# Prompt scores from high and low parts, decode rows regrouped, and memory updates of two batch elements side by side

## The chip, the cores and the metric

The program runs on one core of a Trainium2 chip. The metric is the device time of one launch in microseconds (us), the median of three runs. TensorE (PE) does the matrix products, VectorE (DVE), ScalarE (ACT) and GpSimd (POOL) do the elementwise work, and SyncE (SP) issues most of the DMAs. Each engine takes its instructions in order. They are tied together by semaphores: an instruction adds to one, and another engine waits until it has reached a number.

## The reference

One decoder layer for 256 prompt tokens and 8 x 4 decode tokens (288 columns in all), model width 2048, in fp32. Only the second sub-layer matters here:

```
x += 1/2 * post_norm(SwiGLU_1(pre_norm(x)))
p  = pre_norm(x) @ w_in           # q, k, v, o of 4 heads x 256, two GLU halves, gates
mLSTM per head: s = (q k^T) * w_intra        # prompt: 256 x 256; decode: 4 x 4 in each batch element
                h = (s v + (q C) * w_inter) / max(|den|, exp(-m))
                C_new = g_state * C + sum_s g_keys k_s v_s^T      # decode: for each of 8 batch elements
conv:  GLU -> causal depthwise conv (31 taps) -> LayerNorm -> swish
x += post_norm(concat[heads, conv] @ w_out)
x += 1/2 * post_norm(SwiGLU_2(pre_norm(x)))
```

## The kernel before

**The stream.** Everything is held feature-major: 128 features on the partitions, 288 tokens along a row. All weights come as 654 pieces of 128 x 1024 in four slots. For a piece, ACT makes its high part `whi` (rounded to fp32r, L910), and DVE or POOL makes the rest `wlo` by a subtraction (`split_lo`: L1330 on DVE, L1860 on POOL; `DVE_LO` at L105 says which pieces of the middle stage are DVE's). PE multiplies each 128 x 128 block in three products: high by high, high by low, low by high (L473 to L475, `multiply`). 24 of these make one piece. A tile of the result (two pieces in the middle stage) lies in one of four PSUM banks until DVE takes it out (`evict`, L1515), and PE must find the bank free when it starts the tile four further on.

**The middle stage.** For each piece p of it, PE, ACT, DVE and POOL each run a list written out by hand. For head h the place is k = p - `KEYS_AT[h]`, with `KEYS_AT` = 8, 30, 54, 78. On PE, `between(p, j)` puts small products behind block j of piece p, here written (k, j). On DVE the order within a piece is: evict, LayerNorm part, head part, gate part, convolution part, and the split last. ACT's is: split, then the parts. Heads 1 and 2 have the same pattern. In head 0, the convolution's taps (L1624) run on DVE up to k = 13. In head 3, the LayerNorm steps of the conv channels run beside it (`ln_part`, `ln_squares` on PE, L780).

**One head.** The tiles k0, k1, v0, v1, q0, q1 come at k = 0 to 11. At k = 8 ACT copies the decode columns of keys and values four times side by side (`kv4`, L1158), so that 128 partitions hold four copies of the 32 decode rows. PE turns them (k = 9). At k = 10 ACT and at k = 11 DVE make of these copies high and low parts `k4`, `v4`: rows of one copy hold the high part, rows of another the low part (L1169 to L1171, L1674, L1678), and a product over all 128 rows then gives the sum of the products of parts. At k = 12 and 13 ACT makes `vm`: for each of 8 batch elements the values with all other rows zeroed (L1189). At k = 12 DVE evicts q1 and weights the queries (`qw`, `qwn`, L1687 to L1696). PE's `scores` follow at (13, 5), (13, 1), (13, 1), (13, 3) in heads 0 to 3: four fp32 products for the prompt, two of 256 columns and two of 128, each recorded as two instructions (L687), and two products of 32 columns for the decode tokens (L690). `query_memory` (L705) multiplies into four groups of 32 columns of the array, 16 fp32 products recorded as 32. `attend` (L728) waits among others for DVE's L1717.

**The memory update.** `update_memory(h, b)` multiplies `k4` by `vm` of batch element b: two fp32r products over all 128 rows, of 256 columns each (L744), into bank 7 or 4 in turn. It runs eight times, three blocks apart from (16, 1) to (18, 6), in head 0 two pieces later and in head 3 three (`LATE`). It waits until the bank's last content, two updates back, is out. DVE adds each to the memory `C` (L1737): numbers 0, 1, 2 at k = 16, 3 and 4 at k = 17, 5, 6, 7 at k = 18 (plus `LATE`), always behind that piece's `evict`.

## Time and profile before

| | |
|---|---|
| median of three runs | 2156.44 us (2156.44 to 2157.05) |
| the profiled execution | 2157.24 us, of which the span of the trace is 2155.5 us |
| instructions | 41798 |
| PE busy | 2149.3 us, 16278 products |
| DVE, ACT, POOL busy | 972.9, 895.1, 961.7 us |
| granted TensorE clock | 1.00 |
| DMA | 376.63 MB, mean 175 GB/s |

The busy time of an engine is the union of its instructions' durations. A product on PE overlaps the next, so its duration (some 0.30 us for 288 columns) is not what it costs; the distance from its start to the next start is (0.13 us). The timeline gives start, duration, engine, line and operation. Where one engine runs several instructions of one line in a row, they stand as one row with their count. "[... <- X]" is the idle time before it and what ended it.

### The profile page before, as it was taken

The numbers are of one execution on the slowest core, as the hardware profiler recorded it, in microseconds if no ns is written. First come the engines' busy times: TensorE is split into PE (matmuls) and PEld (weight loads), VectorE is DVE, ScalarE is ACT, GpSimd is POOL, SyncE is SP. The second block draws the span as 40 slices with busy tenths as digits, with TensorE's granted clock in tenths as the row PEclk, the third lists the DMA queues.
The fourth block names the chain that finished last, engine by engine and source line by source line (L and its number), as shares of the span: only waits on it lengthen the run. The fifth ranks groups of instructions, "written<-read, shape, count | busy, mean of one in ns | idle before, by whom it ended". The sixth has DMA issues, their size and how long they took to land.

```text
span 2155.5 us, 41798 instructions
## 1 busy us (share of the span) xinstructions
PE 2149.3 (100%) x16278; PEld 2138.5 (99%) x16278; DVE 972.9 (45%) x1406; ACT 895.1 (42%) x1159; POOL 961.7 (45%) x563
## 2 busy tenths in 40 slices
PE   9999999999999999999999999999999999999999
PEld 9999999999999999999999999999999999999998
DVE  6533432223434224987659738533432223333323
ACT  6434333333343335644345446433333333333443
POOL 1444443334444445466756332444443334444444
PEclk9999999999999999999999999999999999999999
DMA  7454555455555554656656544545455545554653
GB/s 249 165 168 163 165 166 172 159 165 168 167 164 162 170 169 146 208 191 229 239 191 226 194 160 148 172 160 171 156 172 168 167 157 170 162 172 157 210 164 129
DMA packets 104692, 376.63 MB, mean 175 GB/s; under 512 B 11640, under 2 KB 15868, under 8 KB 103584
## 3 DMA queue, kind: packets, MB, share of 16 engines
q1 hardware_dynamic: 97632, 349.00, 49.0%
q10 hardware_dynamic: 6848, 26.37, 3.5%
q8 instruction: 62, 1.02, 0.2%
q14 instruction: 22, 0.18, 0.0%
q0 software_dynamic: 128, 0.07, 0.0%
HBM read 360.21 MB, written 15.18 MB: 174 GB/s over the span
## 4 chain that ended last, share of the span: by engine, by line
PE 99%; DVE 1%; issue 0%; ACT 0%; POOL 0%; DVEq 0%; POOLq 0%
PE bank L475 30%; PE bank L473 30%; PE bank L474 30%; PE bank L528 1%; PE bank L535 1%; PE bank L539 1%; PE bank L833 1%; PE bank L835 1%; PE bank L834 1%; PE bank L546 0%; PE bank L744 0%; PE bank L770 0%; PE bank L687 0%; DVE wlo L1330 0%; DVE prod L1636 0%; PE bank L728 0%
## 5 line engine op out<-in xcount | busy, mean ns | idle before, releaser
L1860 POOL TENSOR_TENSOR wlo<-raw,whi 128x1024 fp32r<-128x1024 f32 x331 | 796.6, 2408 | 850.5 <-ACT whi L910 770.7
L473 PE MATMUL bank<-xh,whi 128*128 128x288 f32 x3344 | 992.1, 297 | 0.0
L474 PE MATMUL bank<-xl,whi 128*128 128x288 f32 x3344 | 988.3, 296 | 0.0
L475 PE MATMUL bank<-xh,wlo 128*128 128x288 f32 x3344 | 986.4, 295 | 0.0
L910 ACT ACTIVATE whi<-raw 128x1024 fp32r<-128x1024 f32 x652 | 687.3, 1056 | 604.8 <-PE bank L475 560.8
L1330 DVE TENSOR_TENSOR wlo<-raw,whi 128x1024 fp32r<-128x1024 f32 x323 | 467.7, 1449 | 771.2 <-ACT whi L910 769.9
L473 PEld LDWEIGHTS bank<-xh,whi 128*128 128x128 f32 x3344 | 630.2, 188 | 2.4 <-issue 2.2
L475 PEld LDWEIGHTS bank<-xh,wlo 128*128 128x128 f32 x3344 | 629.8, 188 | 0.0
L474 PEld LDWEIGHTS bank<-xl,whi 128*128 128x128 f32 x3344 | 628.7, 188 | 0.2
L475 PE MATMUL bank<-hh,wlo 128*128 128x288 f32 x1408 | 417.4, 296 | 0.0
L473 PE MATMUL bank<-hh,whi 128*128 128x288 f32 x1408 | 416.1, 296 | 0.0
L474 PE MATMUL bank<-hl,whi 128*128 128x288 f32 x1408 | 410.5, 292 | 0.0
L474 PEld LDWEIGHTS bank<-hl,whi 128*128 128x128 f32 x1408 | 268.4, 191 | 0.0
L473 PEld LDWEIGHTS bank<-hh,whi 128*128 128x128 f32 x1408 | 264.5, 188 | 0.0
L475 PEld LDWEIGHTS bank<-hh,wlo 128*128 128x128 f32 x1408 | 263.8, 187 | 0.0
L1883 POOL TENSOR_TENSOR scr<-scr 128x288 f32<-128x288 f32 x88 | 74.7, 849 | 208.7 <-ACT scr L999 208.7
L1003 ACT ACTIVATE hh<-scr 128x288 f32 (+1 forms) x88 | 39.1, 444 | 275.6 <-DVE scr L1468 275.6
L999 ACT ACTIVATE scr<-scr 128x288 f32<-128x288 f32 x88 | 39.2, 445 | 220.7 <-DVE scr L1447 220.7
L1447 DVE TENSOR_TENSOR scr<-bank,rstd 128x288 f32<-128x288 f32 x176 | 80.3, 456 | 77.1 <-PE bank L475 72.3
L1624 DVE SCALAR_TENSOR_TENSOR bank<-upad,vec,bank 128x256 f32<-128x256 f32 x232 | 92.8, 481 | 0.1
L1873 POOL TENSOR_TENSOR ssq<-ssq,sq 128x288 f32<-128x288 f32 x45 | 36.5, 812 | 79.3 <-ACT sq L1060 54.2
L1470 DVE TENSOR_TENSOR hl<-scr,hh 128x288 f32 (+1 forms) x88 | 40.3, 458 | 64.0 <-ACT hh L1003 64.0
(265 smaller groups left out, 1271.4 us busy)
## 6 DMA issues: line engine op xcount, KB each, us to landing
raw<-stream SPq DMA_DIRECT2D x654, 512.0 KB, 3.5
C<-c_in ACTq DMA_DIRECT2D x4, 2048.0 KB, 8.2
cs_out<-C ACTq DMA_DIRECT2D x4, 2048.0 KB, 7.9
late_kv<-late ACTq DMA_DIRECT2D x1, 2048.0 KB, 13.5
y_out<-x_res SPq DMA_DIRECT2D x7, 288.0 KB, 2.2
bc<-row_copy ACTq DMA_DIRECT2D x4, 448.0 KB, 8.6
conv_out<-upad ACTq DMA_DIRECT2D x4, 302.0 KB, 5.0
upad<-conv_in ACTq DMA_DIRECT2D x4, 272.0 KB, 3.4
```

Of the source, the lines that this page charges most:

```text
L473: pe.matmul(out, wh, mov_hi[:, k, :], start=first, stop=False)
L474: pe.matmul(out, wh, mov_lo[:, k, :], start=False, stop=False)
L475: return pe.matmul(out, wl, mov_hi[:, k, :], start=False, stop=last)
L910: act.activation(whi[:, g % SLOTS, :], raw[:, g % SLOTS, :], ACT.Copy).then_inc(hi_ready, 1)
L999: act.activation(scr[:, 2, :], scr[:, f % 2, :], ACT.Sigmoid).then_inc(sig_ready, 1)
L1003: act.activation(hh[:, k, :], scr[:, 4, :], ACT.Copy).then_inc(h_hi, 1)
L1330: dve.tensor_tensor(wlo[:, g % SLOTS, :], raw[:, g % SLOTS, :], whi[:, g % SLOTS, :].bitcast(F32), ALU.subtract).then_inc(lo_ready[g % SLO ...
L1447: ins = dve.tensor_tensor(out, src, rstd[:, :], ALU.mult)
L1470: dve.tensor_tensor(hl[:, k, :], scr[:, 4, :], hh[:, k, :].bitcast(F32), ALU.subtract)\
L1624: ins = dve.scalar_tensor_tensor(out=out, in0=up_prompt(j, SEQ, k), scalar=w, in1=acc, op0=ALU.mult, op1=ALU.add)
L1860: pool.tensor_tensor(wlo[:, g % SLOTS, :], raw[:, g % SLOTS, :], whi[:, g % SLOTS, :].bitcast(F32), ALU.subtract).then_inc(lo_ready[g % SL ...
L1883: pool.tensor_tensor(scr[:, 5 + f % 2, :], scr[:, f % 2, :], scr[:, 2, :], ALU.mult)\
```

## The change

The scores of the prompt take high and low parts of keys and queries: ACT writes the high parts `qk_hi` (`keep_high`, keys at k = 8, queries at k = 12), DVE subtracts them in place (`keep_low`, keys at k = 10, queries at k = 12), and PE makes three fp32r products for each fp32 product before. The copies of the decode rows are laid out per batch element (16 rows each: four copies of four tokens) in place of four copies of all 32. High and low rows are then told by masks `side` and `colv`, made once ahead, and the parts of `k4` and `v4` come from one instruction each over all rows. `vm` has two entries in place of eight, each with one batch element in every group of 32 rows. The update takes two batch elements at a time, each with a product over its own 32 rows, in two groups of array rows, four times in a head. Constants on POOL and DVE ahead of the heads, and the split of one small DMA into two, go with it.

```diff
+PAR = NB // Q_GROUP
+COPIES = P // NS
+UPDATE_ORDER = (0, 2, 1, 3, 4, 6, 5, 7)
...
             def scores(h):
                 pe.wait_ge(tile_evicted, tile_of(h, "q1") + 1)
                 pe.wait_ge(dec_lo, h + 1)
-                k, q = qkvo[:, 1, :, :], qkvo[:, 0, :, :]
+                for n in range(2):
+                    pe.wait_ge(qk_low[n], h + 1)
                 for lo, n, s, l in ((0, SEQ, 0, 0), (SEQ, P, P, P)):
                     for c in range(DC):
-                        pe.matmul(bank[7][:, lo:lo + n], k[:, c, s:s + P], q[:, c, l:l + n], start=(c == 0),
-                                  stop=(c == DC - 1))
+                        for m, (ks, qs) in enumerate(((qk_hi, qk_hi), (qk_hi, qk_lo), (qk_lo, qk_hi))):
+                            pe.matmul(bank[7][:, lo:lo + n], ks[:, 1, c, s:s + P], qs[:, 0, c, l:l + n],
+                                      start=(c + m == 0), stop=(c == DC - 1 and m == 2))
...
-            def update_memory(h, b):
-
-                if b < 2:
-                    pe.wait_ge(den_ready if b == 0 else qc_evicted, h + 1)
+            def update_memory(h, n):
+
+                if n:
+                    pe.wait_ge(cu_evicted, NB * h + 2 * n)
                 else:
-                    pe.wait_ge(cu_evicted, NB * h + b - 1)
-                pe.wait_ge(vm_ready, NB * h + b + 1)
-                out = bank[4 if b % 2 else 7]
+                    pe.wait_ge(den_ready, h + 1)
+                    pe.wait_ge(qc_evicted, h + 1)
+                    pe.wait_ge(vm_ready, PAR * (h + 1))
                 for c in range(DC):
-                    mm = pe.matmul(out[:, c * DH:(c + 1) * DH], k4[:, c * P:(c + 1) * P], vm[:, b, :],
-                                   start=True, stop=True)
-                mm.then_inc(cu_done, 1)
+                    for b in UPDATE_ORDER[2 * n:2 * n + 2]:
+                        g, r = divmod(b, PAR)
+                        own_rows = slice(NS * g, NS * (g + 1))
+                        mm = pe.matmul(bank[4 if g % 2 else 7][:, c * DH:(c + 1) * DH], k4[own_rows, c * P:(c + 1) * P],
+                                       vm[own_rows, r, :], start=True, stop=True, tile_position=(NS * g, 0))
+                        if c == DC - 1:
+                            mm.then_inc(cu_done, 1)
...
-            updates = {(16, 1): 0, (16, 4): 1, (16, 7): 2, (17, 2): 3, (17, 5): 4, (18, 0): 5, (18, 3): 6, (18, 6): 7}
+            updates = {(16, 1): 0, (16, 7): 1, (17, 5): 2, (18, 3): 3}
...
-                act.dma_start(row_copy[:, R_GK:ROWS], rowg[:, 0:TOK]).then_inc(rows_stored, 16)
+                act.dma_start(row_copy[:, R_GK:R_GK + SEQ], rowg[:, 0:SEQ]).then_inc(rows_stored, 16)
+                act.dma_start(row_copy[:, R_GK + SEQ:ROWS].rearrange("h (b t) -> h b t", t=NT),
+                              in_copies(rowg[:, SEQ:SEQ + P])[:, :, 0, :]).then_inc(rows_stored, 16)
...
+            def keep_high(h, n):
+
+                act.wait_ge(tile_evicted, tile_of(h, ("q1", "k1")[n]) + 1)
+                if h:
+                    act.wait_ge(sc_done, h)
+                act.activation(qk_hi[:, n, :, :], qkvo[:, n, :, 0:SEQ], ACT.Copy).then_inc(qk_high[n], 1)
...
                     for n in range(2):
-                        last = act.activation(kv4[:, n, :, :].rearrange("p c (j t) -> p c j t", j=P // NS),
-                                              four(qkvo[:, 1 + n, :, SEQ:TOK]), ACT.Copy)
+                        for c in range(DC):
+                            last = act.activation(in_copies(kv4[:, n, c, :]), copied(
+                                qkvo[:, 1 + n, c, SEQ:TOK].rearrange("p (b t) -> p b t", t=NT)), ACT.Copy)
                     last.then_inc(kv4_ready, 1)
+                    keep_high(h, 1)
...
-                if k in (12, 13):
-
+                if k == 12:
+
+                    keep_high(h, 0)
                     act.wait_ge(dec_lo, h + 1)
                     act.wait_ge(mask_ready, 1)
-                    for b in range(4 * (k - 12), 4 * (k - 11)):
-                        act.activation(vm[:, b, :], v4[:, :].bitcast(F32), ACT.Copy, scale=mask[:, b:b + 1])\
+                    for r in range(PAR):
+                        act.activation(vm[:, r, :], v4[:, :].bitcast(F32), ACT.Copy, scale=mask[:, r:r + 1])\
                            .then_inc(vm_ready, 1)
...
+                    dve.wait_ge(side_ready, 1)
+                    for n in range(2):
+                        last = dve.tensor_scalar(colv[:, n, :], col[:, 5, :], side[:, n, 1:2], None, ALU.mult)
+                    last.then_inc(colv_ready, 1)
+                    dve.wait_ge(colv_ready, 1)
                 if k == 11:
 
                     dve.wait_ge(dec_hi, h + 1)
-                    for r in (NS, 3 * NS):
-                        dve.scalar_tensor_tensor(out=v4[r:r + NS, :], in0=bank[7][r:r + NS, 0:DH],
-                                                 scalar=col[r:r + NS, 5, h:h + 1], in1=v4[r:r + NS, :].bitcast(F32),
-                                                 op0=ALU.mult, op1=ALU.subtract)
-                    half = slice(2 * NS, P)
-                    dve.tensor_tensor(k4[half, :], bank[7][half, DH:2 * DH], k4[half, :].bitcast(F32), ALU.subtract)\
-                       .then_inc(dec_lo, 1)
+                    dve.scalar_tensor_tensor(out=v4[:, :], in0=bank[7][:, 0:DH], scalar=colv[:, 0, h:h + 1],
+                                             in1=v4[:, :].bitcast(F32), op0=ALU.mult, op1=ALU.add)
+                    dve.scalar_tensor_tensor(out=k4[:, :], in0=bank[7][:, DH:2 * DH], scalar=side[:, 0, 0:1],
+                                             in1=k4[:, :].bitcast(F32), op0=ALU.mult, op1=ALU.add).then_inc(dec_lo, 1)
+                if k == 10:
+
+                    dve.wait_ge(kg_ready, h + 1)
+                    dve.wait_ge(kv4_ready, h + 1)
+                    keep_low(h, 1)
...
+                    for r in range(PAR):
+                        w = bc[:, h % 2, R_WI:R_GK].rearrange("p (g r t) -> p r g t", r=PAR, t=NT)[:, r, :, :].unsqueeze(1)
+                        last = dve.tensor_tensor(
+                            qw[:, :, r, n * r:n * (r + 1)].rearrange("p c (g t) -> p c g t", t=NT),
+                            qkvo[:, 0, :, SEQ:TOK].rearrange("p c (g r t) -> p c r g t", r=PAR, t=NT)[:, :, r, :, :],
+                            w.broadcast_to([P, DC, Q_GROUP, NT]), ALU.mult)
...
                     dve.tensor_tensor(qwn[:, 0, :], qwn[:, 0, :], qwn[:, 1, :], ALU.add).then_inc(qw_ready, 1)
+                    keep_low(h, 0)
...
-                for b in ((0, 1, 2), (3, 4), (5, 6, 7))[first] if 0 <= first < 3 else ():
-                    dve.wait_ge(cu_done, NB * h + b + 1)
-                    src = bank[4 if b % 2 else 7][:, :]
+                for n in ((0, 1), (2, 3), (4, 5, 6, 7))[first] if 0 <= first < 3 else ():
+                    dve.wait_ge(cu_done, NB * h + n + 1)
+                    b = UPDATE_ORDER[n]
+                    src = bank[4 if b // PAR % 2 else 7][:, :]
...
+            def keep_low(h, n):
+
+                dve.wait_ge(qk_high[n], h + 1)
+                dve.tensor_tensor(qk_lo[:, n, :, 0:SEQ], qkvo[:, n, :, 0:SEQ], qk_hi[:, n, :, :].bitcast(F32),
+                                  ALU.subtract).then_inc(qk_low[n], 1)
```

## Rows read from the trace of the kernel before

**Rows 1.** The profile's page: busy time, share of the span, instructions

```profile
PE 2149.3 (100%) x16278; PEld 2138.5 (99%) x16278; DVE 972.9 (45%) x1406; ACT 895.1 (42%) x1159; POOL 961.7 (45%) x563
```

**Rows 2.** Waits of PE: engine, line, waited for: us in total, times, longest

```profile
PE bank L728 <- DVE sq L1717: 0.4, 2, 0.2
```

**Rows 3.** Groups of PE instructions by form: form, count | busy us, mean ns | idle

```profile
L744 PE MATMUL bank<-vm,k 128*128 128x256 f32 x64 | 12.7, 279 | 0.0
...
L744 PEld LDWEIGHTS bank<-vm,k 128*128 128x128 f32 x64 | 10.2, 188 | 0.0
...
L705 PEld LDWEIGHTS bank<-C,qw 128*32 128x32 f32 x128 | 3.7, 109 | 2.7 <-issue 0.7
```

**Rows 4.** Timeline of PE at the scores of head 0

```profile
930.07 1.47 PE L687 MATMUL bank<-qkvo 128*128 128x256 f32 x8
931.38 0.53 PE L690 MATMUL bank<-qkvo,cpr 128*128 128x32 f32 x4
```

**Rows 5.** Timeline of PE at the first update of head 0

```profile
950.43 0.39 PE L744 MATMUL bank<-vm,k 128*128 128x256 f32 x2
950.67 0.29 PE L473 MATMUL bank<-xh,whi 128*128 128x288 f32 x1
```

**Rows 6.** Timeline of PE around the column-grouped products of head 0

```profile
941.32 0.29 PE L475 MATMUL bank<-xh,wlo 128*128 128x288 f32 x1
941.54 1.93 PE L705 MATMUL bank<-C,qw 128*32 128x256 f32 x32
943.41 0.40 PE L473 MATMUL bank<-xh,whi 128*128 128x288 f32 x1
943.65 0.29 PE L474 MATMUL bank<-xl,whi 128*128 128x288 f32 x1
```

**Rows 7.** One line each: durations ns min/median/max, first and last start, forms

```profile
L1330 DVE TENSOR_TENSOR wlo<-raw,whi x323: 1160/1227/2579, 12.1 to 2126.8; 128x1024 fp32r<-128x1024 f32 x162
L1177 ACT ACTIVATE vtok<-bank x4: 579/580/599, 922.6 to 1173.9; 128x512 f32<-128x512 f32 x4
L1687 DVE TENSOR_TENSOR qw<-qkvo,bc x4: 225/226/1829, 927.2 to 1179.6; 128x64 f32<-128x64 f32 x4
```

**Rows 8.** Timeline of DVE, head 0: before its taps, and k = 10 to 12

```profile
901.63 0.99 DVE L1621 TENSOR_SCALAR bank<-upad,vec 128x256 f32<-128x256 f32 x2 [3.02 <-POOL upad L1995]
...
918.75 3.22 DVE L1624 SCALAR_TENSOR_TENSOR bank<-upad,vec,bank 128x256 f32<-128x256 f32 x8
...
926.72 0.46 DVE L1536 TENSOR_TENSOR qkvo<-bank,rstd 128x288 f32<-128x288 f32 x1
```

**Rows 9.** Timeline of POOL: ahead of the heads, and head 0 at k = 10

```profile
884.76 7.08 POOL L1860 TENSOR_TENSOR wlo<-raw,whi 128x1024 fp32r<-128x1024 f32 x3 [28.81 <-DVE y L1436]
...
918.67 4.79 POOL L1860 TENSOR_TENSOR wlo<-raw,whi 128x1024 fp32r<-128x1024 f32 x2
```

**Rows 10.** Timeline of DVE, head 3, k = 12: eviction of q1, and what follows `qwn`

```profile
1179.07 0.46 DVE L1536 TENSOR_TENSOR qkvo<-bank,rstd 128x288 f32<-128x288 f32 x1
...
1180.26 1.22 DVE L1330 TENSOR_TENSOR wlo<-raw,whi 128x1024 fp32r<-128x1024 f32 x1
```

**Rows 11.** Timeline of PE: scores and first update of head 1, scores of head 3

```profile
1007.21 1.47 PE L687 MATMUL bank<-qkvo 128*128 128x256 f32 x8
...
1023.27 0.40 PE L744 MATMUL bank<-vm,k 128*128 128x256 f32 x2
...
1179.96 1.47 PE L687 MATMUL bank<-qkvo 128*128 128x256 f32 x8
```

**Rows 12.** Timeline of DVE: head 1 at k = 12 and 18, head 0 at k = 18

```profile
1003.44 0.46 DVE L1536 TENSOR_TENSOR qkvo<-bank,rstd 128x288 f32<-128x288 f32 x1 [2.77 <-PE bank L475]
...
1030.94 0.46 DVE L1525 TENSOR_TENSOR scr<-bank,rstd 128x288 f32<-128x288 f32 x1 [0.76 <-POOL upad L1995]
1031.32 0.74 DVE L1737 SCALAR_TENSOR_TENSOR C<-C,bc,bank 128x512 f32<-128x512 f32 x1
...
954.40 1.22 DVE L1330 TENSOR_TENSOR wlo<-raw,whi 128x1024 fp32r<-128x1024 f32 x1
```

More of the change, by code:

```diff
@@ L228, in hybrid_layer_kernel @@
         ml = place("ml", [P, D_MLSTM // P, TOK], F32R)
+        qkvo_at = arena[0]
         qkvo = place("qkvo", [P, 4, DC, TOK])
+        qk_lo = place("qk_lo", [P, 2, DC, TOK], F32R, qkvo_at)
         yc = place("yc", [P, CC, TOK])
@@ L272, in hybrid_layer_kernel @@
         ntmp = place("ntmp", [P, DC, NB])
-        mask = place("mask", [P, NB])
+        mask = place("mask", [P, PAR])
+        side = place("side", [P, 2, 2])
+        colv = place("colv", [P, 2, H])
         qwn = place("qwn", [P, DC, NS])
@@ L346, in hybrid_layer_kernel @@
         cap_ready, cap_added = sem("cap_ready"), sem("cap_added")
+        qk_high, qk_low = [sem(f"qk_high{n}") for n in range(2)], [sem(f"qk_low{n}") for n in range(2)]
+        low_ready, side_ready, colv_ready = sem("low_ready"), sem("side_ready"), sem("colv_ready")
         turn_ready, sums_ready = sem("turn_ready"), sem("sums_ready")
@@ L800, in between @@
                         attend(h)
-                    b = updates.get((k - LATE[h], j))
-                    if b is not None:
-                        update_memory(h, b)
+                    n = updates.get((k - LATE[h], j))
+                    if n is not None:
+                        update_memory(h, n)
                 if (p, j) == (MIX_FROM, 3):
@@ L1136, in head_part @@
                 if h == 0 and k == 6:
[L1138 removed]
+                    act.wait_ge(rows_stored, 48)
                     spread_rows(0)
@@ L1607, in _ @@
             dve.wait_ge(cap_ready, 1)
-            dve.tensor_reduce(ntmp[:, 0, :].rearrange("p (r j) -> p r j", j=Q_GROUP), own, AX_X, ALU.add)
+            dve.tensor_reduce(ntmp[:, 0, :].rearrange("p (g r) -> p g r", r=PAR), own, AX_X, ALU.add)
             link(dve.tensor_reduce(turn[:, 1:2], cap[:, :], AX_X, ALU.max))
@@ L1611, in _ @@
             dve.tensor_scalar(turn[:, 1:2], turn[:, 1:2], 0.0, None, ALU.is_ge).then_inc(turn_ready, 1)
+            dve.wait_ge(low_ready, 2)
+            dve.tensor_reduce(side[:, 0, 0:1], low16[:, :], AX_X, ALU.add)
+            link(dve.tensor_reduce(side[:, 0, 1:2], low8[:, :], AX_X, ALU.add))
+            dve.tensor_scalar(side[:, 1, :], side[:, 0, :], -2.0, 1.0, ALU.mult, ALU.add).then_inc(side_ready, 1)
             def tap(h, j, k):
@@ L1980, in _ @@
                     pool.wait_ge(pool_chain, 4)
+            for low, n in ((low8, 4), (low16, 8)):
+                pool.memset(low[:, :], 1.0).then_inc(pool_chain, 1)
+            pool.wait_ge(pool_chain, 6)
+            for low, n in ((low8, 4), (low16, 8)):
+                pool.affine_select(out=low[:, :], in_=low[:, :], compare_op=ALU.is_ge, fill=0.0, base=-n,
+                                   pattern=[[-2 * n, P // (2 * n)]], channel_multiplier=1).then_inc(pool_chain, 1)
+            pool.wait_ge(pool_chain, 8)
+            for low, n in ((low8, 4), (low16, 8)):
+                pool.affine_select(out=low[:, :], in_=low[:, :], compare_op=ALU.is_ge, fill=0.0, base=2 * n - 1,
+                                   pattern=[[2 * n, P // (2 * n)]], channel_multiplier=-1).then_inc(low_ready, 1)
             pool.wait_ge(xsq_sum, 2)
```

79 lines of the change are left out of this document (42 added, 37 removed).

## The prediction

> **What bounds the kernel now.** I read the page first: PE is busy for 2149.3 us of the 2155.5, the other engines for under half [rows 1]. PE's waits come next, and there is one pair of 0.2 us behind DVE's L1717 in heads 1 and 2 [rows 2]. So PE never stops, and an edit counts only in two ways: by how far it moves the starts of the products that follow, and by waits on PE that are new. Waits need the timelines of DVE, ACT and POOL beside PE's, head by head, because the slack at each of the places changed is different: that is the third view. The profiled execution took 2157.24 us, 0.8 above the median of the runs (2156.44). My sum starts from 2157.24 and I take off 0.8 at the end. Half of the question is which side of plus or minus 4.3 us the result lies on, since under 0.2% this kernel's measurement can't be told from no change.
>
> **Scores on PE.** Four fp32 products take 1.31 us from the first start to that of L690 [rows 4]. Their columns are as many as six instructions of 256 would have (four of 256, four of 128), so an fp32 instruction of 256 columns costs 0.218 us. In their place come six fp32r products of 256 columns and six of 128. Of 256 columns I have L744: two in 0.24 us, so 0.12 each, 0.72 for six [rows 5]. Of 128 columns there is no fp32r product in the trace. If only its columns counted, it would take half, 0.06. But each brings weights of 128 columns. A load of 128 columns takes 188 ns and one of 32 takes 109 [rows 3]: 79 ns for 96 columns, so 105 ns for 128, and loads that follow one another can't be closer. Six by 0.105 are 0.63 us, the sum is 1.35, and that is 0.04 more than before in a head, **+0.2 us** in four. Ends: 0.06 each gives 1.08 and -0.9 us in all; the rate of fp32 (0.218 for a product of 128 columns, two such instructions) gives 2.03 and +2.9 us. I take the load's rate, as it is measured on this engine's own weights.
>
> **Updates on PE.** Before, eight times 0.24 us in a head, 64 instructions in all [rows 3, 5]: 1.92 us a head. After, four groups, each of two times two products with 32 rows. If the two run side by side a group takes 0.24. But the array is divided otherwise for it, and back again. The trace has this for columns: L705's 32 instructions of 256 columns run four at a time, which is 8 x 0.218 = 1.75 us. They take 1.87 to the next start, the step into them is 0.22 where 0.13 is usual, and the step behind the next product is 0.24 [rows 6]: 1.87 + 0.09 + 0.11 - 1.75 = 0.32 us for going in and out. So a group costs 0.24 + 0.32 = 0.56, four cost 2.24, and that is 0.32 a head more than before: **+1.3 us**. What is saved in a head (0.96) is paid back by four divisions. Ends: no price for dividing gives 0.96 a head, -3.8 us in all; loads that don't overlap (4 x 0.105 = 0.42) and the full price give 0.74 a group, +4.2 us. I take the price of rows 6 because it is the same engine going over to groups and back.
>
> The Trainium skill, TensorEngine Tiling, Key Properties, states that changing the tiling mode, and not merely the tile, drains the engine. The trace agrees, with the 0.32 us of rows 6; by this rule alone the term is the one I took.
>
> **Scores' new wait.** PE now waits for `keep_low(h, 0)`. Behind q1's eviction stand: on ACT `keep_high` (512 columns, as L1177, 0.58 us [rows 7]), on DVE the weighting of the queries, then `keep_low`, half of L1330's 1.23, so 0.61 [rows 7]. In head 3 DVE was through the weighting 0.73 us after the eviction's end (1179.53 to 1180.26 [rows 10]); with one more small instruction I take 0.95, which covers ACT's 0.58. So the wait can end 0.95 + 0.61 = 1.56 us after the eviction's end. Behind the waiting scores on PE stands everything: the weight stream.
> - Heads 1 and 2: eviction ends at 1003.90 [rows 12], parts ready at 1005.5, scores are due at 1007.21 [rows 11]. Hidden, with 1.7 us left. `keep_low(h, 1)` at k = 10 falls into DVE's idle time there. Cost nothing; without that cover it is what heads 0 and 3 pay.
> - Head 0: DVE runs without a gap here. New ahead of q1: `colv` at k = 7 (two tiny instructions and a wait, some 0.5 us), and `keep_low(0, 1)` at k = 10, 0.61 us of work. It reads two operands in SBUF, and so does POOL's split of 918.67, two of 2.4 us each [rows 9]. How such a meeting goes is seen in L1687, which also reads two: median 0.23 us, and once 1.83, in head 0 [rows 7]. So `keep_low` waits to 921.07 and ends at 921.7, where taps began at 918.75 [rows 8]: 2.9 us late. The decode parts are two instructions instead of three, some 0.4 less. q1 is evicted from 926.72 + 0.5 + 2.9 - 0.4 = 929.7 to 930.2, the parts are ready at 931.8, scores are due at 930.07 [rows 4]: **+1.7 us**. Ends: 0, if DVE gets in between POOL's instructions at once; 4, if one more split of 2.4 us comes first.
> - Head 3: q1's eviction ends at 1179.53 [rows 10], late already, with 0.43 us left to the scores at 1179.96 [rows 11]. `keep_low(3, 1)` adds 0.61 ahead of it and the shorter decode parts take off 0.4; ACT's new copies ahead of the LayerNorm squares add some 0.1. Eviction ends at 1179.85, with 1.56 behind it 1181.4, and hand-overs of 0.1 twice: 1181.6. **+1.7 us**. Ends: 0.5 and 2.6 (POOL's split in the way).
>
> **Updates' new wait.** A group must find both banks out; before, an update waited only for the one two back. Groups are six blocks apart, 18 x 0.1328 = 2.39 us, and 0.56 long: 2.95.
> - Head 1: the first is at 1023.27 [rows 11], the fourth due at 1032.1. It needs the third pair out, and DVE does that at k = 18 only, behind an eviction that itself waits for POOL to 1030.94. L1737 follows at 1031.32 [rows 12]; two at 0.75 end at 1032.8. Wait 0.7 us. Head 2 has the same pattern. Together +1.4.
> - Head 0: the third group is due at 950.43 [rows 5] + 5.90 = 956.3. Number 3 leaves DVE at k = 19, behind a split that runs from 954.40 for 1.22 us [rows 12]: 955.6 + 1.5 = 957.1. Wait 0.8. The fourth is due at 960.05; the eviction at the start of k = 20 (958.5, 0.46 us) and two L1737 end at 960.5. Wait 0.45.
> - Head 3: DVE's splits leave room, and I find no wait.
>
> In all **+2.65 us**; ends 0 (if the fourth pair's order comes out earlier) and 5.
>
> **At nothing.** POOL's new masks: it is idle for 28.81 us behind them [rows 9]. DVE's `side` and the reordered rows: idle for 3.02 us before 901.63 [rows 8]. The second small DMA: issued from ACT's queue, it moves the C load, two stores and the first spreading of the rows by some 0.3 us; head 0's ACT and POOL wait for these rows, but DVE's parts at k = 11 come later than that by more. `vm`, two instead of eight, frees ACT and nobody waits for it. SP's queue is not touched, and no transfer is moved past another. The 0.2 us waits of rows 2 lie between scores and updates, and both sides of them move together.
>
> **Sum.** 0.2 + 1.3 + 1.7 + 1.7 + 2.65 = 7.55. 2157.24 + 7.55 - 0.8 = **2164.0 us**.
>
> **Rivals.**
> 1. *Side by side pays in full, waits stay.* Dividing by rows is free, products of 128 columns run at their columns' rate: -3.8 - 0.9, and the waits' 6.05 remain: +1.35, 2157.8 us, no change. For it: rows' price is from column groups and fp32, and each division there loads four sets of weights first. Against it: 0.22 for 0.13 on the way in is seen every time. The Trainium skill, TensorE: Matmul & The Clock Gate, Measured speedup vs the span model, gives 3.07x for four row groups, so nearly this; no run here shows it.
> 2. *Faster: the waits vanish.* Place: DVE at k = 10 and 12 of heads 0 and 3. If POOL gives way at once and the parts are there when the scores come, and DVE has both banks out in time, only PE's -4.7 is left: 2151.7 us. It decides when DVE gains about 1.7 us in these two heads. Against it: DVE has no gap in head 0, and only 0.43 us to spare in head 3.
> 3. *PE worse than taken.* Products of 128 columns at fp32's rate, and the loads of a group in series: +2.9 + 4.2 + 6.05 = 13.15, 2169.6 us.
> 4. *The change does little.* PE's terms cancel and half of the waits is hidden by the pieces ready ahead: +3, 2159.4 us.
>
> **How the numbers follow.** My case 0.42, rival 1 0.17, rival 2 0.12, rival 3 0.13, rival 4 0.16. Below 2152.1 is faster: 0.12. Above 2160.8 is slower: 0.42 + 0.13 and the upper end of rival 4: 0.60. Between: 0.28. The range leaves out the tails of rivals 2 and 3: 2153 to 2170. My case alone spans 2160 to 2168.
>
> **What would show it.** Scores: L687's successor, 48 instructions, from first start to L690's in 1.35 us (1.08 or 2.03 in the other cases). Updates: from a group's first start to the next product's, and the step behind it, 0.56 in place of 0.24. New rows among PE's waits: for DVE's `keep_low` in heads 0 and 3, 1.7 us each, and none in heads 1 and 2; for L1737's successor, 0.7 to 0.8 us, three or four times, none in head 3. `keep_low(0, 1)` at some 2.9 us where half of 1.23 is its own. The forecast is wrong if PE shows no waits, or a group takes under 0.4 us.

## The result, and the profile after

The changed kernel takes 2168.93 us (median of 4 runs, 2167.15 to 2170.16), the kernel before 2156.61 in the same rounds. The ratio is 1.0056 (95% interval 1.0045 to 1.0068), so it is slower, by 12.3 us. The forecast was 2164.0 with a range of 2153 to 2170. The profiled execution took 2167.15 us and its span is 2165.4, 9.9 longer than before.

The page of the changed kernel, busy time, share of the span and instructions:

```profile
PE 2153.9 (99%) x16294; PEld 2137.8 (99%) x16294; DVE 979.0 (45%) x1419; ACT 890.6 (41%) x1151; POOL 960.8 (44%) x569
```

PE is busy for 4.6 us more than before [rows 1] and idle for 5.3 more. Its waits (engine, line, waited for: us in total, times, longest) say where the idle time is. Before there were three lines here: those for `ident` and `rpost`, as below, and the one for `sq` [rows 2]:

```profile
PE bank L708 <- DVE qk_lo L1798: 3.8, 2, 3.4
PE bank L565 <- POOL ident L1992: 1.7, 1, 1.7
PE bank L768 <- DVE C L1790: 1.1, 3, 0.4
PE bank L749 <- DVE sq L1769: 0.4, 2, 0.2
PE bank L688 <- ACT cpr L1193: 0.2, 1, 0.2
PE bank L795 <- ACT rpost L1348: 0.2, 1, 0.2
```

L708 is the scores' line now (L687 before), L768 the updates' (L744), L1798 `keep_low`, L1790 the update of C (L1737). Two of the three new waits were forecast: scores behind `keep_low`, twice, and updates behind C, three times. Head 0's scores wait twice as long as forecast. The third, 0.2 us at L688, was not forecast: PE turns the decode rows of head 0 and waits for ACT's copies of them.

**Scores of head 1**, where nothing waits (timeline of PE: start, duration, instruction):

```profile
1013.03 0.28 PE L708 MATMUL bank<-qk_hi 128*128 128x256 f32 x1
1013.15 0.28 PE L708 MATMUL bank<-qk_lo,qk_hi 128*128 128x256 f32 x1
...
1013.92 0.27 PE L708 MATMUL bank<-qk_hi,qk_lo 128*128 128x128 f32 x1
...
1014.36 0.47 PE L711 MATMUL bank<-qkvo,cpr 128*128 128x32 f32 x3
```

From first start to the next line's it is 1.33 us, where the four fp32 products took 1.31 [rows 4]. A product of 256 columns takes 0.12, and one of 128 columns 0.11 (1013.92 to 1014.36 is four of them): the shorter one is hardly faster. That fits the 0.105 us that the prediction estimated for loading 128 columns of weights.

**The first updates of head 0**, the same view:

```profile
955.20 0.29 PE L494 MATMUL bank<-xh,wlo 128*128 128x288 f32 x1
955.42 0.50 PE L768 MATMUL bank<-vm,k 32*128 32x256 f32 x4
955.85 0.40 PE L492 MATMUL bank<-xh,whi 128*128 128x288 f32 x1
956.09 0.30 PE L493 MATMUL bank<-xl,whi 128*128 128x288 f32 x1
```

The group takes 0.43 to the next start. The step into it is 0.22 and the one behind the next product 0.24, where 0.13 is usual: 0.43 + 0.09 + 0.11 = 0.63 us for two batch elements, against 2 x 0.24 = 0.48 one after the other [rows 5]. The step out is the same as behind the groups by columns [rows 6].

**The scores of head 0.** PE, then the engines' work in five stretches (window, its length, busy time of PE, PEld, DVE, ACT, POOL with counts, granted clock as a share of 2.4 GHz, DMA share, GB/s):

```profile
929.58 0.29 PE L494 MATMUL bank<-xh,wlo 128*128 128x288 f32 x1
933.26 0.36 PE L708 MATMUL bank<-qk_hi 128*128 128x256 f32 x1 [3.39 <-DVE qk_lo L1798]
...
935.52 0.59 PE L492 MATMUL bank<-xh,whi 128*128 128x288 f32 x1
```

```profile
926.40:929.58 3.18, 3.18 (x27) 3.18 (x25) 3.18 (x10) 0.00 (x0) 2.70 (x2) 1.00 0.98 317
929.58:932.97 3.39, 0.29 (x3) 0.05 (x1) 3.29 (x13) 1.42 (x4) 0.00 (x0) 1.00 0.62 202
932.97:935.52 2.55, 2.26 (x17) 2.29 (x17) 2.38 (x7) 0.96 (x2) 1.51 (x1) 0.82 0.02 6
935.52:938.10 2.58, 2.58 (x12) 2.58 (x13) 2.04 (x7) 0.70 (x1) 0.85 (x1) 0.52 0.20 37
938.10:941.00 2.90, 2.90 (x24) 2.90 (x24) 2.83 (x3) 2.13 (x4) 2.46 (x1) 1.00 0.39 148
```

Two things are to be seen. PE stands still for 3.39 us. And behind that the granted clock is 0.82 and then 0.52, the lower level (1.2 GHz) for most of the time from 934.7 to 938: 12 products in 2.58 us where the stretch ahead has 27 in 3.18. I come to 1.6 us lost in it, an estimate from the shifts of equal products on either side.

Why the parts come so late is in the timeline of DVE, with POOL's below it:

```profile
907.80 3.65 DVE L1712 TENSOR_SCALAR colv<-col,side 128x4 f32<-128x4 f32 x2
...
921.25 0.45 DVE L1574 TENSOR_TENSOR qkvo<-bank,rstd 128x288 f32<-128x288 f32 x1
921.62 2.48 DVE L1798 TENSOR_TENSOR qk_lo<-qkvo,qk_hi 128x512 fp32r<-128x512 f32 x1
...
931.08 0.44 DVE L1574 TENSOR_TENSOR qkvo<-bank,rstd 128x288 f32<-128x288 f32 x1
...
932.32 0.68 DVE L1798 TENSOR_TENSOR qk_lo<-qkvo,qk_hi 128x512 fp32r<-128x512 f32 x1
```

```profile
904.31 7.11 POOL L1919 TENSOR_TENSOR wlo<-raw,whi 128x1024 fp32r<-128x1024 f32 x3 [1.16 <-ACT whi L935]
...
918.77 4.78 POOL L1919 TENSOR_TENSOR wlo<-raw,whi 128x1024 fp32r<-128x1024 f32 x2
921.11 2.44 POOL L1919 TENSOR_TENSOR wlo<-raw,whi 128x1024 fp32r<-128x1024 f32 x1
```

`colv`, two instructions on 4 columns, takes 3.65 us, and it ends at 911.45 where POOL's three splits end at 911.42. `keep_low` takes 2.48 beside POOL's splits and 0.68 at 932.32, where POOL is idle. q1's eviction starts at 931.08, where 929.7 was forecast.

How long head 0's scores wait is not fixed. The edits of experiments 4 and 5 lie behind these scores in the program, so up to them their code is the changed kernel's. Their traces show waits of 2.17 and 1.76 us, with `colv` at 3.65 and 3.56 and `keep_low(0, 1)` at 1.13 and 0.68 in place of 2.48. The second one:

```profile
921.30 0.68 DVE L1804 TENSOR_TENSOR qk_lo<-qkvo,qk_hi 128x512 fp32r<-128x512 f32 x1
931.29 0.36 PE L708 MATMUL bank<-qk_hi 128*128 128x256 f32 x1 [1.76 <-DVE qk_lo L1804]
```

So between executions of the same code this wait differs by up to 1.6 us, by how `keep_low` falls between POOL's splits. All that follows on the size of the wait has to be read with that.

The span, by the shifts of equal products between the two traces: at 882 us the changed kernel is 0.8 ahead, which is no effect of the change (the first products of the span alone lie up to 0.8 apart from one kernel to the next, with the same work). From there it loses 0.4 before head 0's scores (at L688), 5.2 at them (wait 3.5, clock 1.6, products 0.1), 3.7 at the four heads' updates, 0.3 at the scores of heads 1 to 3 themselves, and 1.0 by waits in head 3, of which 0.7 at the scores with their hand-over and 0.3 earlier, at the LayerNorm squares. Unrounded that is 10.7, and with 0.8 taken off the 9.9 of the span.

### The profile page after: what moved, and what is told of

Same layout as the page of the kernel before. It is cut to its first block, busy times and chain, and to the rows that moved or that the text cites. A ratio compares the mean times of both kernels' runs of the same rounds, so it can differ in the third digit from the quotient of the medians.

```text
span 2165.4 us, 41825 instructions
## 1 busy us (share of the span) xinstructions
PE 2153.9 (99%) x16294; PEld 2137.8 (99%) x16294; DVE 979.0 (45%) x1419; ACT 890.6 (41%) x1151; POOL 960.8 (44%) x569
## 4 chain that ended last, share of the span: by engine, by line
PE 95%; DVE 3%; issue 1%; POOL 1%; ACT 0%; POOLq 0%; DVEq 0%; ACTq 0%
PE bank L494 29%; PE bank L492 29%; PE bank L493 28%; PE bank L547 1%; PE bank L558 1%; PE bank L554 1%; DVE bank L1664 1%; PE bank L858 1%; PE bank L860 1%; PE bank L859 1%; POOL wlo L1919 0%; PE bank L565 0%; DVE wlo L1368 0%; PE bank L795 0%; PE bank L708 0%
```

## The experiments

All are edits of the changed kernel. The kernel before took 2156.44 us (16 runs) beside experiments 1 to 4 and 2156.59 (21 runs) beside 5 to 7. The last column counts the executions by the mean of their granted clock.

| kernel | median us (lowest to highest) | ratio to before, 95% | span | wait at head 0's scores | mean clock of the executions |
|---|---|---|---|---|---|
| changed | 2168.93 (2167.15 to 2170.16) | 1.0056 (1.0045 to 1.0068) | 2165.4 | 3.39 | 1 at 0.999, 3 at 0.998 |
| `colv` from PSUM | 2167.56 (2163.33 to 2167.85) | 1.0043 (1.0029 to 1.0056) | 2165.8 | 2.35 | 2 at 1.000, 3 at 0.998 |
| PE kept at work | 2165.76 (2165.36 to 2167.25) | 1.0044 (1.0030 to 1.0058) | 2163.9 | filled | 5 at 1.000 |
| fp32 scores | 2160.96 (2160.56 to 2161.71) | 1.0021 (1.0012 to 1.0030) | 2159.4 | none | 11 at 1.000 |
| updates one by one | 2162.69 (2160.32 to 2165.99) | 1.0031 (1.0019 to 1.0044) | 2159.3 | 2.17 | 2 at 1.000, 1 at 0.999, 3 at 0.998 |
| one form per head | 2164.27 (one execution) | | 2162.5 | 1.76 | 1 at 1.000 |
| everything mended | 2161.07 (2160.53 to 2165.17) | 1.0023 (1.0014 to 1.0032) | 2159.5 | 1.43 | 10 at 1.000, 1 at 0.998 |
| fp32 scores, other order | 2159.37 (2159.05 to 2159.86) | 1.0013 (1.0004 to 1.0022) | 2157.5 | none | 11 at 1.000 |

The last column sorts the spread. The kernels whose scores never wait (before, and both with fp32 scores) show 1.000 in every execution and lie within 1.2 us. The changed kernel shows less than 1.000 in all four. In experiment 1 the two executions at 1.000 took 2163.3 and 2164.2 and the three at 0.998 took 2167.6 to 2167.9; in experiment 4 it is 2160.3 and 2161.1 against 2163.7 to 2166.0, in experiment 6 at most 2161.3 against one of 2165.2. So the executions with a lower mean clock take some 3 to 5 us more, and whether the lower level comes differs from one execution of a kernel to the next.

**1. `colv` read from PSUM.** Is the 3.65 us a meeting with POOL over SBUF, and is it what made head 0's scores late?

```diff
-  last = dve.tensor_scalar(colv[:, n, :], col[:, 5, :], side[:, n, 1:2], None, ALU.mult)
+  last = dve.tensor_scalar(colv[:, n, :], bank[7][:, 5 * H:6 * H], side[:, n, 1:2], None, ALU.mult)
...
   pe.wait_ge(col_ready, 1)
+  pe.wait_ge(colv_ready, 1)
```

The second part keeps PE from overwriting bank 7 before `colv` has read it.

> The changed kernel (2168.93 us, its profiled execution 2167.15), with one edit: the two tiny colv instructions of head 0 read the columns from the PSUM bank instead of SBUF. Theory (they stood 3.65 us behind POOL's splits, because they and POOL both read SBUF over one way): they take under 0.5 us; DVE is 3.2 us earlier, of which 0.9 is lost again because keep_low(0, 1) then meets POOL's split of 918.8 and ends at 921.8 instead of 924.1. PE's wait for the scores of head 0 falls from 3.39 to about 1.1 us, the stretch at the low clock behind it (935 to 938, 1.6 us lost) is gone, and the time falls by about 3.9 us to 2165.0. Rival (DVE meets POOL anyway, at the next instruction): the wait stays above 2.5 us, the low clock stays, gain under 1 us.

The first half is shown: the same arithmetic, with the values of `col` read from PSUM and `side` from SBUF as before, takes a tenth of the time, beside the same splits of POOL (the experiment's DVE):

```profile
908.15 0.35 DVE L1713 TENSOR_SCALAR colv<-bank,side 128x4 f32<-128x4 f32 x2
...
919.98 2.88 DVE L1799 TENSOR_TENSOR qk_lo<-qkvo,qk_hi 128x512 fp32r<-128x512 f32 x1 [1.23 <-POOL scr L2090]
```

The second half stays open. Of the 3.3 us that `colv` is shorter, 1.25 are left at q1's eviction (929.83 for 931.08). DVE now comes to `keep_low(0, 1)` early and waits for POOL's gate of the keys, which in turn waited for the rows of `bc`; the experiment's POOL:

```profile
918.17 0.25 POOL L2083 TENSOR_TENSOR wt<-bc,cap 128x32 f32<-128x32 f32 x1 [2.27 <-DMA bc<-row_copy]
918.38 1.58 POOL L2090 TENSOR_TENSOR scr<-qkvo,bc 128x288 f32<-128x288 f32 x2
```

Of the 2 us lost on the way, 1.2 are that wait and 0.4 a longer `keep_low`. But the wait is hardly an effect of the edit: the rows of `bc` landed 1.15 us later in this execution than in the changed kernel's (POOL's `wt` starts at 918.17 for 917.02; over the nine traces it is 916.9 to 918.4). With the earlier time POOL's gate would have ended at 918.8, as DVE came free. Why they land later is not shown.

The scores still wait 2.35 us, not 1.1. As the same code without this edit waited 1.76 to 3.39, the trace doesn't tell what the edit took off the wait. The clock still falls, and for twice as long as in the changed kernel:

```profile
932.00:938.80 6.80, 6.65 (x29) 6.68 (x30) 4.95 (x13) 2.04 (x3) 2.58 (x2) 0.50 0.40 143
```

That is why the span is no shorter with a wait shorter by 1.0 us. By the medians the edit is worth 1.4 us where 3.9 was expected, and 1.7 by the medians of the executions at 0.998.

**2. PE kept at work while it waits.** Is the slower stretch behind the wait an effect of the idle time? Work is added and none taken away:

```diff
+  if h == 0:
+      keep_warm(14, bank[7])
   for n in range(2):
       pe.wait_ge(qk_low[n], h + 1)
```

> The changed kernel with 14 products of ones (fp32, 128 columns, 0.22 us each, into the bank that the scores overwrite) on PE ahead of head 0's wait for the low parts: 3.05 us of work that nobody needs, in a wait of 3.39. Theory (PE's clock fell from its upper to its lower level because PE stood idle for 3.39 us): the granted clock stays at 1.00 throughout, the products behind the scores keep 0.13 us, and the time falls by 1.6 us or somewhat more, to 2167.0, though work was added. The spread of the runs (2167.2 to 2170.2) shrinks too, if it came from the length of the slow stretch. Rival (the clock falls for another reason, or the wait merely grows by the added work): same time as the changed kernel or later, low clock still there.

The clock does not fall. The experiment's PE, the last `keep_low` ahead of the scores, and two windows of 4 us:

```profile
930.12 3.39 PE L565 MATMUL bank<-ones 128*128 128x128 f32 x28
933.26 0.36 PE L710 MATMUL bank<-qk_hi 128*128 128x256 f32 x1
```

```profile
931.00 0.68 DVE L1800 TENSOR_TENSOR qk_lo<-qkvo,qk_hi 128x512 fp32r<-128x512 f32 x1
```

```profile
930.00:934.00 4.00, 3.88 (x34) 3.88 (x35) 3.90 (x13) 2.38 (x4) 1.82 (x2) 1.00 0.63 231
934.00:938.00 4.00, 4.00 (x34) 4.00 (x34) 2.71 (x8) 1.76 (x2) 1.57 (x2) 1.00 0.34 131
```

The scores start at 933.26, as in the changed kernel, but by chance: the parts were ready at 931.7 here, and it is the added work that holds the scores for the last 1.3 us or so. So this trace does not fill a wait of 3.39 us, but one of some 2 us (an estimate). The weight lies on the executions: all five have a mean clock of 1.000, where the four of the changed kernel have 0.999 and 0.998. Here, work in the idle time kept the clock up.

Added work made the span 1.5 us shorter and the median 3.2. With equal starts of the scores, the first is the clock's 1.6. The median gains more because the changed kernel's profiled execution, at 0.999, lost the least. Over some 2165 us, its stretch of 3.4 us at half the clock makes a mean of 0.9992, one of 6.8 us as in experiment 1 makes 0.9984, and the three other executions stand at 0.998. No trace of those exists, so that their stretch was so long is an estimate; it makes 1.7 us more.

**3. Scores in fp32 again.** This splits the change in two: `keep_high`, `keep_low` and the twelve products go, the rows' order and the updates stay.

```diff
-  for m, (ks, qs) in enumerate(((qk_hi, qk_hi), (qk_hi, qk_lo), (qk_lo, qk_hi))):
-      pe.matmul(bank[7][:, lo:lo + n], ks[:, 1, c, s:s + P], qs[:, 0, c, l:l + n], ...)
+  pe.matmul(bank[7][:, lo:lo + n], qkvo[:, 1, c, s:s + P], qkvo[:, 0, c, l:l + n], ...)
...
-  keep_high(h, 1)
...
-  keep_low(h, 1)
...
```

> The changed kernel with the prompt's scores as four fp32 products from the whole keys and queries again, and keep_high and keep_low left out; the new order of the decode rows, colv and the updates in pairs stay. Theory (the scores' part costs 3.55 for the wait in head 0, 1.6 for the clock, 0.98 for head 3's two waits, 0.07 to 0.14 a head for the products): the time falls by 6.4 us to 2162.5; no wait at the scores; the groups of updates unchanged at 0.63 us each. Rival (colv's 3.65 us is enough to make DVE late in head 0): a wait of over 1 us stays there, and the time is 2164 or more.

The time is 2160.96, 1.5 lower than expected. Of the 12.3 us, 8.0 hang on the scores and their parts, 4.4 on the updates and what is common. PE's waits here (columns as above):

```profile
PE bank L765 <- DVE C L1779: 1.1, 3, 0.4
...
PE bank L734 <- DVE scr L1753: 0.2, 1, 0.2
```

`colv` still takes 3.64 us in this kernel, and no scores wait. With the parts away, a new wait shows in head 0 (L734, 0.2 us), and experiment 7, with the same `colv`, has none there. So `colv` alone costs PE at most this 0.2 us; more it costs only with `keep_low` between it and q1. The updates' 1.1 is the same with either kind of scores.

**4. Updates one at a time.** Eight single updates of 128 rows at eight places, as before the change. `vm` still has two entries, so each product adds up four batch elements and the new memories are not the right ones; the work on PE is that of single updates.

```diff
-  own_rows = slice(NS * g, NS * (g + 1))
-  mm = pe.matmul(bank[...], k4[own_rows, c * P:(c + 1) * P], vm[own_rows, r, :], ..., tile_position=(NS * g, 0))
+  mm = pe.matmul(bank[4 if n % 2 else 7][:, c * DH:(c + 1) * DH], k4[:, c * P:(c + 1) * P], vm[:, n % 2, :], ...)
...
-  updates = {(16, 1): 0, (16, 7): 1, (17, 5): 2, (18, 3): 3}
+  updates = {(16, 1): 0, (16, 4): 1, (16, 7): 2, (17, 2): 3, (17, 5): 4, (18, 0): 5, (18, 3): 6, (18, 6): 7}
```

> The changed kernel with the updates one at a time again, eight a head in the places that they had before, each over all 128 rows; scores in three products stay. vm still has two entries, so the new memories are sums over four batch elements (that part of the result is changed). Theory (updates in pairs cost 0.63 us for 0.48, and their waits for banks 0.3, 0.45 and 0.45): the time falls by 3.7 us to 2165.2, groups of 0.24 us, no wait at the updates. Rival (what was lost lies in the scores alone, and the pairs are as fast as single updates): less than 1.5 us.

The updates' waits are gone, the median is 6.2 us lower, more than expected. In the profiled execution head 0's scores wait 2.17 us, and the clock stays at 1.00 through 926 to 942. The six runs lie apart, 2160.3 to 2161.7 and 2163.7 to 2166.0, and the upper three are those with a mean clock of 0.998. The shorter span (6.1) is made of 1.2 less wait at the scores, 1.6 of the clock and 3.3 of the updates, and 16 groups at 0.15 with 1.1 of waits are 3.5. Only the last belongs to this edit. The wait is shorter because `keep_low(0, 1)` fell otherwise between POOL's splits and took 1.13 us instead of 2.48. This run therefore bears out the updates' share, but not by its median.

**5. One form of update per head.** What does a group's 0.63 consist of? Head 0 as in the changed kernel; head 1 with both products of a pair in the same group of rows; head 2 with all 128 rows (sums over four batch elements, so its new memories are not the right ones); head 3 with the products of one batch element behind one another.

```diff
-  for c in range(DC):
-      for b in UPDATE_ORDER[2 * n:2 * n + 2]:
+  for c, m in ([(c, m) for m in range(2 * n, 2 * n + 2) for c in range(DC)] if h == 3 else
+               [(c, m) for c in range(DC) for m in range(2 * n, 2 * n + 2)]):
+      b = m if h == 1 else UPDATE_ORDER[m]
...
+      if h == 2:
+          mm = pe.matmul(out, k4[:, c * P:(c + 1) * P], vm[:, r, :], start=True, stop=True)
```

> The changed kernel with the groups of updates in another form in each head: head 0 as it is (pairs in different row groups, 0.43 us from first start to the next product's, and 0.20 more at the two steps around it, 0.63 in all); head 1 with both of a pair in the same row group (batch elements 0 and 1, 2 and 3, and so on, banks chosen so that they fit); head 2 with all 128 rows in each product (sums over four batch elements, so the new memories of that head are changed); head 3 as head 0, but the two products of one batch element behind one another. Theory (two row groups do run side by side, and 0.39 is the price of dividing): head 1 needs 0.24 more, 0.87 a group; head 2 loses the division, 0.48; head 3 lies between 0.63 and 0.87. Rival (loads of 128 columns, 0.105 each, set the pace and nothing runs side by side): head 1 is as head 0, 0.63, and head 3 too.

One group each of heads 1, 2 and 3, from the experiment's timeline of PE (head 0 repeats the group shown above, at 0.43):

```profile
1025.47 0.29 PE L494 MATMUL bank<-xh,wlo 128*128 128x288 f32 x1
1025.69 0.73 PE L774 MATMUL bank<-vm,k 32*128 32x256 f32 x4
1026.35 0.40 PE L492 MATMUL bank<-xh,whi 128*128 128x288 f32 x1
...
1112.94 0.29 PE L494 MATMUL bank<-xh,wlo 128*128 128x288 f32 x1
1113.07 0.63 PE L771 MATMUL bank<-vm,k 128*128 128x256 f32 x4
1113.54 0.29 PE L492 MATMUL bank<-xh,whi 128*128 128x288 f32 x1
...
1210.58 0.29 PE L866 MATMUL bank<-xh,wlo 128*128 128x288 f32 x1
1210.81 0.51 PE L774 MATMUL bank<-vm,k 32*128 32x256 f32 x4
1211.24 0.40 PE L864 MATMUL bank<-xh,whi 128*128 128x288 f32 x1
```

Start to next start the four heads have 0.43, 0.66, 0.47 and 0.43 us; the step in is 0.22 or 0.23 in all but head 2, where it is 0.13. Head 1 came as expected (0.86 with the steps) and so did head 2. So the products of different row groups do run side by side, 0.43 against 0.66 in one group. But that 0.66 is already more than 0.47, the price of the same four products with all rows. Side by side saves 0.23, of which 0.19 only makes good what a 32-row product costs more, and going in and out adds 0.20. The order inside a group makes no difference (head 3); I had expected something between, and that was wrong.

The Trainium skill, TensorE: Matmul & The Clock Gate, section "Measured speedup vs the span model", gives 3.07x for four row groups. No run here has four row groups. For two, with products of 256 columns, the trace gives less: two row groups gain 0.66 / 0.43 = 1.5x over one, 0.47 / 0.43 = 1.1x over the undivided array, and 0.48 / 0.63 = 0.8x with the divisions.

**6. Everything mended that can be.** `colv` from PSUM as in 1; C's evictions in the order that the groups want; and in heads 0 and 3 both `keep_low` at k = 12, behind q1's eviction and ahead of the weighting of the queries.

```diff
-  for n in ((0, 1), (2, 3), (4, 5, 6, 7))[first]
+  for n in ((0, 1), (2, 3, 4, 5), (6, 7))[first]
...
-  if k == 10:
+  if k == 10 and h in (1, 2):
...
   dve.wait_ge(tile_evicted, tile_of(h, "q1") + 1)
+  if h in (0, 3):
+      dve.wait_ge(kg_ready, h + 1)
+      dve.wait_ge(kv4_ready, h + 1)
+      keep_low(h, 1)
+      keep_low(h, 0)
```

> The changed kernel with all its new waits attacked at once, the computation unchanged: colv from the PSUM bank; updates 4 and 5 brought in by DVE at k = 17, ahead of k = 18's eviction; in heads 0 and 3 both subtractions of low parts at k = 12 right behind the eviction of q1, ahead of the weighting of the queries, so that DVE doesn't meet POOL's split behind kg at k = 10. Theory (what the change costs beyond its waits is 0.6 us a head for the groups and 0.07 to 0.14 for the scores, some 2.8 in all, and 0.4 ahead): waits at the scores under 0.5 us together, none at the updates, clock 1.00, time 2156.44 + 3.2 + 0.5 = 2160.1. Rival (the waits only change places): above 2163.

2161.07 us, 7.9 less than the changed kernel and still 4.5 more than before. The updates' waits are gone, head 3's is down to 0.15, and the clock stays in ten of eleven executions. Left is head 0, 1.43 us, where under 0.5 was expected for all heads together. Its eviction is early now; DVE and POOL of this kernel:

```profile
925.45 0.45 DVE L1575 TENSOR_TENSOR qkvo<-bank,rstd 128x288 f32<-128x288 f32 x1
925.93 4.76 DVE L1805 TENSOR_TENSOR qk_lo<-qkvo,qk_hi 128x512 fp32r<-128x512 f32 x2
930.62 2.46 DVE L1741 TENSOR_TENSOR qw<-qkvo,bc 128x32 f32<-128x32 f32 x2
```

```profile
924.95 7.97 POOL L1926 TENSOR_TENSOR wlo<-raw,whi 128x1024 fp32r<-128x1024 f32 x3
```

The two `keep_low` take 2.0 and 2.9 us, about the time of a split on POOL each, where 0.68 was seen with POOL idle. They go on in step, one of DVE's to one of POOL's. Alone they would have been through at 927.3 by my estimate (2 x 0.68), well ahead of the scores. So the order of DVE's work was not what stood in the way here; the two engines' meeting was. For `keep_low` that rests on the rows of several kernels; a run with POOL's splits moved away was not made.

**7. fp32 scores and the other order.** The updates' change alone, with its waits mended.

```diff
   (the edit of 3, and)
-  for n in ((0, 1), (2, 3), (4, 5, 6, 7))[first]
+  for n in ((0, 1), (2, 3, 4, 5), (6, 7))[first]
```

> The run with fp32 scores (2160.96) and the fourth pair's wait taken away by the same order of DVE's additions (4 and 5 at k = 17). Theory: the three waits of 0.28, 0.41 and 0.42 us are gone, and 1.1 us comes off: 2159.9. What is left over the kernel before, some 3.4 us, is the price of the groups, 16 x 0.15 = 2.4, and what lies ahead of the heads. Rival (DVE held at k = 17 for the third group delays an eviction or a split of its own, and a wait of the same size comes up elsewhere): 2160.8 or more.

2159.37: the order gives 1.6 us against experiment 3 (1.1 was expected), and no update waits any more. What is left over the kernel before is 2.8 us. 16 groups at 0.63 - 0.48 = 0.15 are 2.4 of it, and the shift at L688, 0.3 here, is most of the rest. Without any wait at the updates, the pairing itself costs. No edit here gave a version that beats the kernel before.

## Why the prediction was right, and where it was not

The direction, most places and most of the mechanism were right: PE was full before, and nearly every cost is either a longer group on PE or a new wait at a place named. What was not in it at all is the clock and the wait at L688. The time lies inside the range, 4.9 us above the forecast and 0.9 above what my own case was to span. By the terms of the sum:

| term | forecast | measured |
|---|---|---|
| scores on PE, four heads | +0.2 | +0.1, with the steps around them +0.4 |
| a group of updates on PE; in all | 0.56; +1.3 | 0.63; +2.4 |
| head 0's wait | +1.7 | +3.5 (1.8 and 2.2 in experiments 5 and 4) |
| the clock behind it | not seen | +1.6 |
| head 3's wait | +1.7 | +0.7, and 0.3 ahead of it |
| heads 1 and 2 | 0 | 0 |
| updates' waits | +2.65 | +1.1 |
| ahead of head 0's scores | 0 | +0.4 |

Luck has a part in the number: head 0's wait, the clock, the groups, L688 and the scores' steps came 5.1 us higher than forecast, the updates' waits and head 3's 2.3 lower. These are the terms of the profiled execution; the median lies 1.8 above it.

**Right by its working.** The load's rate for 128 columns: 0.105 forecast, 0.11 measured, so the scores took 1.33 us for 1.35; neither the column rate (1.08) nor the fp32 rate (2.03) holds. `keep_low(0, 1)` was to make DVE 2.9 us late: it took 2.48, in step with POOL. Heads 1 and 2 hide theirs.

**The step that failed most** is "`colv` at k = 7 (two tiny instructions and a wait, some 0.5 us)". It took 3.65, and 3.56 to 3.65 in every other trace in which it reads `col` from SBUF. Experiment 1 shows that reading the values from PSUM ends that. It does not show that two operands in SBUF are the reason, as `side` still comes from there, and other rows speak against it. The convolution's taps read two operands in SBUF as well, `upad` and a column of `vec`, and keep their 0.40 us from one to the next beside a split [rows 8, 9]. And instructions with a single operand in SBUF were held up beside POOL's splits too, the first of these in the kernel before, the second in the changed one:

```profile
895.76 1.68 DVE L1604 COPY mout<-mrun 4x8 f32<-4x8 f32 x1
```

```profile
897.27 1.74 DVE L1651 TENSOR_SCALAR side<-side 128x2 f32<-128x2 f32 x1
```

Like `colv`, both take one tensor from SBUF and write to SBUF. The first of these rows was the one that should have warned. Which property of these instructions decides is open.

It would not have been a matter of size alone: experiment 3 shows that 3.65 us at k = 7 are all but hidden when no `keep_low` follows. And the forecast wait of 1.7 came true in experiment 5's trace (1.76) with `colv` at 3.56, because `keep_low(0, 1)` took 0.68 there and was not held up: two misses that cancel. What delays head 0 is the sum of `colv`, `keep_low(0, 1)` and the work behind q1's eviction.

The Trainium skill, SBUF — State Buffer, section "SBUF: two separate sides", states that a DVE instruction with two SBUF inputs and a GpSimd one that reads SBUF exclude each other, whoever comes first holding the ports for its whole instruction. For `keep_low`, which subtracts one tensor in SBUF from another, the traces agree: 2.48 us in the changed kernel and 2.0 and 2.9 in experiment 6 beside splits, 0.68 with POOL idle.

**The clock** was no term at all. In the traces it fell behind idle times of PE of 3.39 us (changed kernel) and 2.35 (experiment 1), and not behind 2.17 (experiment 4), 1.76 (experiment 5) or 1.43 (experiment 6). But a kernel's traced wait doesn't decide it: four of six executions of experiment 4 and one of eleven of experiment 6 have a mean clock below 1.000, and two of five of experiment 1 don't (what the scores waited in them is not on record). So it can't be said that the clock would have stayed with the forecast wait of 1.7. A wait of this size should have carried a term for it, with a chance and some 1.6 to 4 us, and my upper end of 4 us for the wait all the more.

**The group of updates.** The division's price, taken from the column groups [rows 6] as 0.32, is 0.20 for row groups (0.22 in, 0.24 out, as there; the groups by columns lose 0.12 inside as well). The products themselves were taken as fully side by side, 0.24, and took 0.43, close to the serial loads' end that I had put at 0.42. That nearness is no proof of serial loads: in one row group the same four took 0.66. Two misses of opposite sign, +0.19 and -0.12, leave +0.07 a group, 1.1 us in all. Experiment 5 shows both parts apart.

**The updates' waits** came at the fourth group in heads 0, 1 and 2 (0.28, 0.41, 0.41), not at the third and fourth of head 0, and some 0.6 times as long. A group that takes 0.07 longer, with everything behind it, gives DVE time; that this is the reason is not shown. That all of them could be ordered away is shown by experiment 7.

**Head 3.** Forecast at 1.7, and 0.43 us of it seen at the scores. Its q1 was evicted late, at 1186.93, 7.9 later than before [rows 10], but PE, behind the delays of three heads, was due 8.7 later (1188.69 for 1179.96 [rows 11]). The gap between them had grown by 0.9 us, and the wait is smaller by as much. The slack of a late head can't be read off without the delays of the heads ahead. That PE loses 0.3 at the LayerNorm squares instead was not in my list.

**Rivals.** Rival 1 (row groups free) falls with the group's 0.63, rival 2 (the waits vanish) with PE's waits. Of rival 3 neither half holds: fp32's rate is refuted by the 1.33 us of the scores, loads in series by the 0.66 of one row group, though their price for two (0.42) is nearly the measured one. Of rival 4 nothing: no piece that was ready ahead covered a wait in head 0.

## What to carry to other kernels

Where TensorE is full, four small products in two row groups are worth less than the same products undivided as long as the group is entered and left each time: count the two steps around it, and compare with the undivided form, not with one row group. A small DVE instruction that takes its tensors from SBUF is to be looked up in the trace beside POOL's work before it is costed by its size: copies and subtractions of this kind waited out POOL's current instruction here, the taps did not, and reading the values from PSUM took the wait away. A new wait of some 2 us or more on a busy TensorE is to be priced with a chance of the slower clock behind it. And where a wait depends on how two engines' instructions happen to meet, one trace of a kernel does not give its size: look at every trace that has the same code up to there.

## What the runs showed of the hardware that I had not expected

- Two DVE instructions on 4 columns took 3.65 us with the values in SBUF and 0.35 us with them in PSUM, beside the same work of POOL. A copy of 4 x 8 from SBUF to SBUF took 1.68 us beside POOL's split, while the taps, which read a tensor and a column in SBUF, took 0.47 to 0.49 us each throughout.
- The granted clock was 0.50 for 3.4 us behind an idle time of 3.39 us and for 6.8 us behind one of 2.35. Of kernels with waits of 1.4 to 2.4 us at this place in their traces, some executions kept 1.000 and others did not; with work in the idle time all five kept it.
- Products of 32 rows cost more than products of 128 rows of the same columns: 0.66 us against 0.47 for four. The order of row groups within the four made no difference (0.43 either way).
- fp32r products of 128 columns follow one another at 0.11 us, those of 256 at 0.12. Three of them for one fp32 product (two instructions; 0.216 us each at 256 columns and 0.111 at 128, by their starts in the trace of the kernel before) are 0.35 for 0.43 at 256 columns and 0.33 for 0.22 at 128: the long rows gain what the short ones lose.
